# Four mixing-gate units and the two state-gate and four state-projection units move into the attention of a three-block fp32 kernel

## The chip, the cores and the metric

The kernel runs on one core of a Trainium2 chip. The metric is the device time of one execution in microseconds (us). The engines of the core run their own instruction queues side by side and wait for one another on semaphores: TensorE (PE) multiplies matrices, VectorE (DVE), ScalarE (ACT) and GpSimd (POOL) work elementwise, SyncE (SP) issues the weight loads.

## The reference

Input is a sequence of 256 tokens of width 1024, all in fp32. The change lies in the first block:

```
h   = rmsnorm(x);  hp = h @ w_in        # u | q | kv | gate logits | 2 x 1024 mixing gates
y_ssm = s5_mixer(u)                     # 32 groups x 64 complex states, a scan over 256 tokens,
                                        # then gelu, and out = yg * sigmoid(yg @ w_glu + b_glu)
y_nsa = nsa_mixer(q, kv, gate logits)   # 8 heads, 2 kv groups: compressed (15 blocks),
                                        # selected and windowed attention, three softmaxes
gate  = sigmoid(mixing gates)
merged = gate[0] * (y_ssm @ w_proj_ssm) + gate[1] * (y_nsa @ w_proj_nsa)
x = x + merged @ w_out
x = x + relu(rmsnorm(x) @ w_up)**2 @ w_down
```

Two more layers follow (feed-forward, retention or latent attention, memory attention, feed-forward); only the product of the memory with its key and value weights (`mem_w_kv_2`, here `w_mem`) is computed already in the first block. The change touches nothing behind the first block.

## The kernel before

**Units.** All weights come in units of up to 1 MB, in the order of the list `UNITS`; SP loads unit n into slot n mod 4 of `raw` as soon as unit n-4 is used up. A split unit is multiplied in three passes so that the result has fp32 accuracy: ACT rounds the weights into `whi` (line 582), DVE subtracts to get `wlo` (line 1033), and PE multiplies high by high, low by high and high by low (line 1825, 48 matmuls of 256 columns for a full unit, 24 for a half unit such as `w_glu`, `w_ps`, `w_pn`). `whi` and `wlo` have two slots each, so the splitting of a unit waits until the unit two before it is multiplied. `ensure` and `ahead` in ACT's and DVE's queues write these splits into the queues by hand. `w_mem` and `w_c1` units aren't split. PE writes unit results in turn into banks 0 and 1 of PSUM, and DVE empties them (`fill_result`).

**State loop.** 16 state tiles j, in 8 pairs p. Per tile DVE turns the inputs by cosine and sine (lines 1179, 1180), adds (`zin`, lines 1213, 1214), scans (`zz`, line 1218), and POOL turns the two scans back in four products (`pr`, lines 1742, 1743). PE does `inputs(p+1)` (line 1942), then `outputs(p-1)` (line 1953), which waits until POOL is through with both tiles of the pair before; POOL may start the next pair only behind these outputs. Between them PE has one unit per tile (`fill(FILL[j])`): 16 of them, the second `w_q`, three `w_kv`, eight `w_mg` (mixing gates), four `w_mem`. `keys_values` (lines 1970 to 1977) stands before the last fill.

**Between loop and attention.** PE compresses the blocks of keys and values (line 2004), computes the gate logits (line 2016) and small products, then `w_glu` 0 and 1 on `yghi`/`yglo`, waits for the sigmoid and the split of the gated output (`yshi`, `yslo`, line 1270), and multiplies the four `w_ps`.

**Attention.** 12 parts (`sub`) of 4 heads each, in groups of three (selected, windowed, compressed), and `values` behind each group (line 2074). PE's order is: scores of part k+2, transposes of part k, values. DVE reads the scores (`prep`: lines 1292, 1297, 1303), ACT takes the exponentials (line 745), DVE normalises (`norm`), PE transposes, ACT copies to SBUF (`copies`, line 755). Scores have one set of banks, so scores of the next part wait until `prep` has read those before. Parts 0 to 5 belong to the first 128 queries (128 keys), parts 6 to 11 to the second (256 keys). After it `yshi`, `yslo` are made from the attention output, and the four `w_pn` units and `w_out` follow.

Of the kernel before, what the change touches and what calls it, by code (L numbers as in the profile page):

```python
# [6 lines left out]
F32 = mybir.dt.float32  # L7
# [4 lines left out]
P = 128  # L12
# [46 lines left out]
def unit_list():  # L59
# [40 lines left out]
AT = {(u[0], u[1]): n for n, u in enumerate(UNITS)}  # L100
NOT_GROUP = ("w_dn", "w_fd", "w_out", "w_o", "w_c1")
# [143 lines left out]
def program(nc, A, out):  # L245

    ctx = ExitStack()
    with ctx:
# [53 lines left out]
        sS = sb("sS", [P, 2, 4 * T], where=[at_yT[0]])  # L302
# [8 lines left out]
        QK = sb("QK", [P, 6, T], where=w)  # L311
        VT = sb("VT", [P, 2, T], where=w)
        KC = sb("KC", [P, 2, T], where=w)
        at_tokens = [w[0]]
        mg = sb("mg", [P, 16, T], where=w)
        xtok = sb("xtok", [P, TT, D], where=at_tokens)
# [24 lines left out]
        yg = sb("yg", [P, 4, T], where=at_ahi)  # L341
        sg = sb("sg", [P, 4, T], where=at_ahi)
        yghi = sb("yghi", [P, 4, T], F32R, where=at_alo)
        yglo = sb("yglo", [P, 4, T], F32R, where=at_alo)
# [17 lines left out]
        cpart = sb("cpart", [P, P], where=at_small)  # L362
        w[0] += 4 * 6 * T
        assert at_small[0] <= w[0]
        sdk = sb("sdk", [P, 2, T], where=w)
        assert w[0] == mark + 3 * half_turn
        mrg = sb("mrg", [P, KT, T], where=w)
        alibi = sb("alibi", [P, NH, T], where=w)
        alibc = sb("alibc", [P, TT, NH, 16], where=w)
        maskc = sb("maskc", [P, TT, HG, 16], where=w)  # L370
        gate = sb("gate", [P, TT, 24], where=w)
# [63 lines left out]

        FILL = {j: AT["w_q", 1] + j for j in range(N_STATE_TILES)}
        assert FILL[N_STATE_TILES - 1] == AT["w_mem", 3]

# [19 lines left out]
        def pre_gain(q):  # L458
# [3 lines left out]
                     nsa=[(alibi, "alibi"), (alibc, "alibc"), (maskc, "maskc"), (xr, "xt")],  # L462
# [107 lines left out]
        def _(act):  # L570
# [122 lines left out]
            act.wait_ge(S("qk_sums"), 1)  # L693
            nc.scalar.activation(rq[:], PS[6][:, 64:80].rearrange("p (a b c) -> p a b c", a=TT, b=HG), ACT.Sqrt,
                                 bias=V["eps"], scale=1.0 / DH).then_inc(S("qk_root"), 1)
            nc.scalar.activation(sdk[:], two(3), ACT.Sqrt, bias=V["eps"], scale=1.0 / DH).then_inc(S("qk_root"), 1)
# [8 lines left out]

            state_gelu(0)
            ensure(SPLIT_BEFORE[AT["w_glu", 0]], AT["w_c1", 1])
            act.wait_ge(*done(AT["w_c1", 1]))
            nc.scalar.activation(cpart[:], PS[7][:, 0:P], ACT.Copy).then_inc(S("cmp_part"), 1)
            act.wait_ge(S("cmp_sum"), 1)  # L710
# [5 lines left out]
            state_gelu(1)  # L716
            act.wait_ge(S("c_done"), N_STATE_TILES)
            for dst, name in SMALL["nsa"]:
                act.dma_start(dst[:], A[name]).then_inc(S("in_nsa"), 16)
            ensure(SPLIT_BEFORE[AT["w_glu", 0]] + 1, AT["w_c1", 1])  # L720
            act.wait_ge(S("gate_logit"), 1)
            nc.scalar.activation(gate[:], gate[:], ACT.Sigmoid).then_inc(S("gate"), 1)
            for c in range(2):
                ahead(AT["w_glu", c])
                act.wait_ge(S("evac"), GROUP[AT["w_glu", c]] + 1)
                nc.scalar.activation(sg[:, 2 * c:2 * c + 2], sg[:, 2 * c:2 * c + 2], ACT.Sigmoid).then_inc(S("ssm_gate"), 1)
            act.wait_ge(S("ys"), 1)
            nc.scalar.activation(yshi[:], yg[:], ACT.Copy).then_inc(S("yshi"), 1)
# [3 lines left out]
            for c in range(4):  # L732
                ahead(AT["w_ps", c])
# [25 lines left out]
            def attention(steps):  # L759
# [10 lines left out]
            nc.scalar.activation(yshi[:], ynf[:], ACT.Copy).then_inc(S("yshi"), 1)  # L770
            for c in range(4):
                ahead(AT["w_pn", c])
# [249 lines left out]
        def _(dve):  # L1022
# [187 lines left out]
            for j in range(N_STATE_TILES):  # L1210
# [9 lines left out]
                if j:  # L1220
# [3 lines left out]
                if j and UNITS[FILL[j - 1]][3]:  # L1224
# [8 lines left out]
            cp(VV[:], PS[2][:, :].rearrange("p (a b c) -> p a b c", a=2, b=TT)).then_inc(S("vv"), 1)  # L1233
            dve.wait_ge(S("qk_root"), 2)
# [8 lines left out]
            state_low(0)  # L1243
            fill_result(FILL[N_STATE_TILES - 1])
            for k in range(2, 4):
                state_output(k)
            ensure(SPLIT_BEFORE[AT["w_glu", 0]], AT["w_c1", 1])
            state_low(1)
# [10 lines left out]

            ensure(SPLIT_BEFORE[AT["w_glu", 0]] + 1, AT["w_c1", 1])  # L1260
            for c in range(2):
                bank = group(AT["w_glu", c])
# [1165 lines left out]
```

## Time and profile before

| | |
|---|---|
| time, median of 3 runs | 1510.44 us (1507.84 to 1510.45) |
| the profiled execution, its own time | 1510.51 us |
| its span (first to last instruction) | 1508.7 us |
| PE / PE weight load busy | 1418.8 / 1374.0 us |
| DVE / ACT / POOL busy | 927.9 / 724.3 / 194.4 us |
| granted TensorE clock, mean | 0.967 of full |

The profile names for each wait what ended it; a chain followed back from the last instruction shows which engine set the end at each moment. Matmuls overlap, so a stretch in which PE counts as busy throughout can still be one of matmuls at half clock; the granted clock is given beside it.

### The profile page before, as it was taken

The numbers are of one execution on the slowest core, as the hardware profiler recorded it, in microseconds if no ns is written. First come the engines' busy times: TensorE is split into PE (matmuls) and PEld (weight loads), VectorE is DVE, ScalarE is ACT, GpSimd is POOL, SyncE is SP. The second block draws the span as 40 slices with busy tenths as digits, with TensorE's granted clock in tenths as the row PEclk, the third lists the DMA queues.
The fourth block names the chain that finished last, engine by engine and source line by source line (L and its number), as shares of the span: only waits on it lengthen the run. The fifth ranks groups of instructions, "written<-read, shape, count | busy, mean of one in ns | idle before, by whom it ended". The sixth has DMA issues, their size and how long they took to land.

```text
span 1508.7 us, 28232 instructions
## 1 busy us (share of the span) xinstructions
PE 1418.8 (94%) x11538; PEld 1374.0 (91%) x11538; DVE 927.9 (62%) x1372; ACT 724.3 (48%) x1193; POOL 194.4 (13%) x210
## 2 busy tenths in 40 slices
PE   5899888799999999999998999999999979899998
PEld 5888777799999999998898999999999977899998
DVE  7998666466644665546765656546665475566544
ACT  7722344354433544435544644436444364654443
POOL 0455100002200011104110211002110010111100
PEclk9899977899999999999999999999999989999999
DMA  9332520344555455554343455554555450255551
GB/s 369 112 141 97 195 84 1 112 160 177 193 196 196 151 184 195 192 195 149 140 154 119 161 183 196 193 196 152 183 205 193 175 193 29 84 181 181 209 193 60
DMA packets 36815, 244.33 MB, mean 162 GB/s; under 512 B 4208, under 2 KB 5360, under 8 KB 8816
## 3 DMA queue, kind: packets, MB, share of 16 engines
q1 hardware_dynamic: 34992, 238.17, 43.8%
q10 hardware_dynamic: 1728, 4.81, 0.9%
q8 instruction: 70, 1.15, 0.3%
q14 instruction: 25, 0.20, 0.0%
HBM read 241.67 MB, written 1.05 MB: 161 GB/s over the span
## 4 chain that ended last, share of the span: by engine, by line
PE 84%; DVE 9%; ACT 4%; issue 1%; DMA 1%; SPq 0%; DVEq 0%; ACTq 0%
PE ps L1825 50%; PE ps L1865 25%; DVE wlo L1033 3%; PE ps L2074 2%; PE ps L2048 1%; ACT whi L582 1%; DVE alo L1414 1%; PE ps L1953 1%; DMA xtok<-in_xt 1%; PE ps L2064 1%; DVE sS L1292 1%; ACT junk L784 1%; DVE yr L1392 0%; ACT pP L745 0%; PE ps L1942 0%
## 5 line engine op out<-in xcount | busy, mean ns | idle before, releaser
L1033 DVE TENSOR_TENSOR wlo<-raw,whi 128x1024 fp32r<-128x1024 f32 (+1 forms) x434 | 506.1, 1208 | 288.7 <-ACT whi L582 288.5
L1825 PE MATMUL ps<-ahi,whi 128*128 128x256 f32 x2112 | 601.5, 285 | 31.7 <-DVE wlo L1033 17.6
L582 ACT ACTIVATE whi<-raw 128x1024 fp32r<-128x1024 f32 (+1 forms) x434 | 427.3, 1032 | 413.7 <-PE ps L1825 217.4
L1825 PE MATMUL ps<-alo,whi 128*128 128x256 f32 x2112 | 596.2, 282 | 0.0
L1825 PE MATMUL ps<-ahi,wlo 128*128 128x256 f32 x2112 | 595.4, 282 | 0.0
L1825 PEld LDWEIGHTS ps<-ahi,whi 128*128 128x128 f32 x2112 | 403.7, 191 | 39.6 <-issue 25.2
L1825 PEld LDWEIGHTS ps<-alo,whi 128*128 128x128 f32 x2112 | 402.8, 191 | 0.7 <-issue 0.7
L1825 PEld LDWEIGHTS ps<-ahi,wlo 128*128 128x128 f32 x2112 | 402.8, 191 | 0.0
L1763 POOL TENSOR_TENSOR hlo<-fh,hhi 128x256 f32 (+3 forms) x104 | 85.7, 824 | 762.0 <-ACT hhi L851 540.9
L1474 DVE TENSOR_TENSOR fa<-ps,r 128x512 f32<-128x512 f32 x104 | 71.9, 692 | 174.3 <-PE ps L1825 174.1
L1865 PE MATMUL ps<-whi,hhi 128*128 128x256 f32 x960 | 147.9, 276 | 0.0
L1865 PE MATMUL ps<-wlo,hhi 128*128 128x256 f32 x960 | 147.9, 276 | 0.0
L1865 PE MATMUL ps<-whi,hlo 128*128 128x256 f32 x960 | 147.8, 276 | 0.0
L1865 PEld LDWEIGHTS ps<-whi,hhi 128*128 128x128 f32 x960 | 126.7, 188 | 0.0
L1865 PEld LDWEIGHTS ps<-whi,hlo 128*128 128x128 f32 x960 | 126.7, 188 | 0.0
L1865 PEld LDWEIGHTS ps<-wlo,hhi 128*128 128x128 f32 x960 | 126.7, 188 | 0.0
L851 ACT ACTIVATE hhi<-fh 128x256 f32 (+1 forms) x88 | 36.8, 418 | 135.1 <-DVE fh L1481 135.1
L1775 POOL TENSOR_TENSOR xr<-xr,yr 128x512 f32<-128x512 f32 x20 | 24.8, 1273 | 327.7 <-PE ps L1885 327.7
L1742 POOL TENSOR_TENSOR pr<-zz,cosT 128x256 f32<-128x256 f32 x32 | 30.7, 958 | 98.9 <-PE ps L1953 58.0
L1481 DVE TENSOR_TENSOR fh<-fs,fa 128x256 f32<-128x256 f32 x88 | 36.9, 419 | 1.9 <-ACT fs L848 1.9
L848 ACT ACTIVATE fs<-fa 128x256 f32<-128x256 f32 x88 | 35.3, 401 | 4.9 <-DVE fa L1474 4.9
L797 ACT ACTIVATE ahi<-ps,vecs 128x128 fp32r<-128x128 f32 x112 | 29.5, 412 | 7.8 <-PE ps L1895 7.8
(344 smaller groups left out, 1392.8 us busy)
## 6 DMA issues: line engine op xcount, KB each, us to landing
raw<-in_w_gu SPq DMA_DIRECT2D x88, 1024.0 KB, 4.8
raw<-in_w_fd SPq DMA_DIRECT2D x44, 1024.0 KB, 4.8
raw<-in_w_up SPq DMA_DIRECT2D x16, 1024.0 KB, 4.8
raw<-in_w_dn SPq DMA_DIRECT2D x16, 1024.0 KB, 4.8
raw<-in_w_ret SPq DMA_DIRECT2D x13, 1024.0 KB, 4.9
raw<-in_w_mg SPq DMA_DIRECT2D x8, 1024.0 KB, 4.8
raw<-in_w_o SPq DMA_DIRECT2D x8, 1024.0 KB, 6.8
raw<-in_w_mem SPq DMA_DIRECT2D x4, 1024.0 KB, 4.8
```

What stands on the lines that cost most here:

```text
L582: nc.scalar.activation(whi[:, m % SPL, c], raw[:, n % RAW, c], ACT.Copy).then_inc(S("w_hi"), 1)
L797: ins = nc.scalar.activation(ahi[:, k, t * P:t * P + P], PS[turned(t, h)][:, i * P:i * P + P], ACT.Copy, scale=pre_gain(q)[:, k:k + 1])
L848: nc.scalar.activation(fs[:, b], fa[:, b, 0:T], ACT.Silu).then_inc(S("silu"), 1)
L851: nc.scalar.activation(dst, fh[:, b, 0:T], ACT.Copy).then_inc(S("hid_hi"), 1)
L1033: ins = tt(wlo[:, m % SPL, c], raw[:, n % RAW, c], whi[:, m % SPL, c].bitcast(F32), ALU.subtract)
L1474: tt(fab, two((g0 + u) % 2), over(r[:, 0:T], 2), ALU.mult).then_inc(S("evac"), 1)
L1481: tt(fh[:, b, 0:T], fs[:, b], fa[:, b, T:2 * T], ALU.mult).then_inc(S("hidden"), 1)
L1742: tt(pr1[:, b, s], zz[:, b, s], cosT[:, j], ALU.mult).then_inc(S("turned"), 1)
L1763: tt(dst, src, high.bitcast(F32), ALU.subtract).then_inc(S("hid_lo"), 1)
L1825: ins = mm(dst, lhsT, rhs, start=k == 0 and p == 0, stop=k == kt - 1 and p == len(pairs) - 1)
L1865: ins = mm(two(2 + 2 * t + c // 2)[:, c % 2], x[:, k, xs], wgt[:, n_slot(n), ws], start=u + kk + p + c % 2 == 0, stop=u == n_units - 1 and ...
L2074: ins = mm(PS[v["bank"]][rows, slot * P:slot * P + P], lhsT, rhs, start=k == 0, stop=k == len(terms) - 1)
```

## The change

It reorders `UNITS` (4 of the 8 `w_mg` and the last `w_mem` go behind), gives 11 instead of 16 tiles of the state loop a unit (`FILL_TILES`: tiles 0 to 4, 6, 8, 10, 11, 12, 14), and puts the others into the attention: `w_mem` 3 between the scores of parts 0 and 1; a table `BESIDE` names the unit that PE multiplies behind the transposes of a part: `w_glu` at parts 0 and 1, `w_ps` at 4 to 7, `w_mg` 4 to 6 at 8 to 10; `w_mg` 7 stands behind the last values. DVE and ACT handle a unit of part n-1 at part n (`beside(n)`). The sigmoid of the state gate reads PSUM directly on ACT. Buffers move to free others (`sS` to the place that `xr` takes later), so that the load of `xr` (`small_in("res")`) now follows the attention, and a wait for it stands ahead of `yslo` on DVE. Functions before the attention on ACT are reordered, with activations on a dummy element that load the next function table (`warm_root`, and those on `warm`).

```
-    add("w_mg", 0, 8)
-    add("w_mem", 0, 4, split=False)
+    add("w_mg", 0, 4)
+    add("w_mem", 0, 3, split=False)
     add("w_c1", 0, 2, split=False)
+    add("w_mem", 3, 1, split=False)
     add("w_glu", 0, 2, 1024)
     add("w_ps", 0, 4, 1024)
+    add("w_mg", 4, 4)
...
+BESIDE = {0: ("w_glu", 0), 1: ("w_glu", 1), 4: ("w_ps", 0), 5: ("w_ps", 1), 6: ("w_ps", 2), 7: ("w_ps", 3),
+          8: ("w_mg", 4), 9: ("w_mg", 5), 10: ("w_mg", 6)}
+FILL_TILES = (0, 1, 2, 3, 4, 6, 8, 10, 11, 12, 14)
...
# ACT
+            act.wait_ge(S("turned"), 4 * N_STATE_TILES)
+            small_in("bias")
...
+            def ssm_gates():
+
+                for c in range(2):
+                    n = AT["w_glu", c]
+                    act.wait_ge(*done(n))
+                    bank = two(GROUP[n] % 2)
+                    for t in range(2):
+                        k = 2 * c + t
+                        ins = nc.scalar.activation(sg[:, k], bank[:, t], ACT.Sigmoid, bias=V["b_glu"][:, k:k + 1])
+                    ins.then_inc(S("evac"), 1)
+
+            def beside(n):
+
+                if n == 0:
+                    ensure(SPLIT_BEFORE[AT["w_glu", 0]] + 1, AT["w_c1", 1])
+                if n - 1 in BESIDE:
+                    ahead(AT[BESIDE[n - 1]])
+                if n == 2:
+                    ssm_gates()
+                if n == 3:
+                    act.wait_ge(S("ys"), 1)
+                    nc.scalar.activation(yshi[:], yg[:], ACT.Copy).then_inc(S("yshi"), 1)
...
                     if n + 1 < len(todo):
                         exps(todo[n + 1])
+                    beside(n)
                     copies(s)
...
             nc.scalar.activation(yshi[:], ynf[:], ACT.Copy).then_inc(S("yshi"), 1)
+            small_in("res")
+            ahead(AT["w_mg", 7])
+            for c in range(4, 8):
+                mix_sigmoid(c)
...
# DVE
+            def beside(n):
+
+                if n == 0:
+                    fill_result(AT["w_mem", 3])
+                    ensure(SPLIT_BEFORE[AT["w_glu", 0]] + 1, AT["w_c1", 1])
+                if n - 1 in BESIDE:
+                    name, c = BESIDE[n - 1]
+                    if name == "w_mg":
+                        fill_result(AT[name, c])
+                    if name == "w_ps":
+                        tt(mrg[:, 2 * c:2 * c + 2], ready(AT[name, c]), mg[:, 2 * c:2 * c + 2], ALU.mult).then_inc(S("evac"), 1)
+                    ahead(AT[name, c])
...
             attention(parts["nsa"], 0)
+            dve.wait_ge(S("in_res"), 16)
             dve.wait_ge(S("yshi"), 2)
             tt(yslo[:], ynf[:], yshi[:].bitcast(F32), ALU.subtract).then_inc(S("yslo"), 1)
+            fill_result(AT["w_mg", 7])
...
# PE
-            pe.wait_ge(S("yglo"), 2)
-            unit(AT["w_glu", 0], yghi, yglo, GLU_KT)
+            outputs(N_STATE_TILES // 2 - 1)
             pe.wait_ge(S("kc_sq"), 1)
...
-            unit(AT["w_glu", 1], yghi, yglo, GLU_KT)
-            pe.wait_ge(S("yslo"), 1)
-            for c in range(4):
-                unit(AT["w_ps", c], yshi, yslo, GLU_KT)
...
                         if k < len(todo):
                             scores(todo[k])
                         transposes(s)
+                        beside(k - 2)
                     else:
                         values(s)
```

The first place is PE's queue in the state loop, the pair of tiles 6 and 7; a unit is shown by its first matmul, `L1942` are the inputs of the next pair, `L1953` the outputs of the pair before. Before:

```order
L1942 MATMUL ps<-uT,BT 128x256 [waits bu_read]
...
L1825 MATMUL ps<-ahi,whi 128x256 [waits w_lo,evac]
...
L1953 MATMUL ps<-pr_96,CD 32x256 [waits turned]
...
L1825 MATMUL ps<-ahi,whi 128x256 [waits w_lo,evac]
...
L1942 MATMUL ps<-uT,BT 128x256 [waits bu_read]
```

After, in the same pair (lines 1993, 1876 and 2004 are the same calls):

```order
L1993 MATMUL ps<-uT,BT 128x256 [waits bu_read]
...
L1876 MATMUL ps<-ahi,whi 128x256 [waits w_lo,evac]
...
L2004 MATMUL ps<-pr_99,CD 32x256 [waits turned]
...
L1993 MATMUL ps<-uT,BT 128x256 [waits bu_read]
```

The unit behind the outputs is gone, so that inputs of the next pair follow the outputs at once.

The second place is DVE's queue at tiles 9 and 10, from the read-out of a mixing-gate unit (`mg`) on. Before:

```order
L1173 TENSOR_TENSOR mg<-ps,r 128x512
L1179 TENSOR_TENSOR t_98<-ps,cosT 128x512
L1180 TENSOR_TENSOR t_99<-ps,sinT 128x512
L1033 TENSOR_TENSOR wlo<-raw,whi 128x1024 x2
L1213 TENSOR_TENSOR zin<-t_98,t_99 128x256
L1214 TENSOR_TENSOR zin<-t_98,t_99 128x256
L1218 SCALAR_TENSOR_TENSOR zz<-sv,zin 128x256 x2
L1173 TENSOR_TENSOR mg<-ps,r 128x512
```

After:

```order
L1215 TENSOR_TENSOR mg<-ps,r 128x512
L1221 TENSOR_TENSOR t_101<-ps,cosT 128x512
L1222 TENSOR_TENSOR t_102<-ps,sinT 128x512
L1255 TENSOR_TENSOR zin<-t_101,t_102 128x256
L1256 TENSOR_TENSOR zin<-t_101,t_102 128x256
L1260 SCALAR_TENSOR_TENSOR zz<-sv,zin 128x256 x2
L1221 TENSOR_TENSOR t_101<-ps,cosT 128x512
```

The weight split and the next read-out are gone from this stretch; of the splits of this loop behind tile 5 one is left, at tile 7.

The third place is PE's queue in the attention, parts 8 to 10 (`L2048` or `L2099` scores, `L2064` or `L2115` transposes, `L2074` or `L2125` values). Before:

```order
L2048 MATMUL ps<-QK 128x256 [waits att_read]
...
L2064 MATMUL ps<-tabs,PC 128x128 [waits att_copy,att_prob]
L2074 MATMUL ps<-pTs,VV 64x128 [waits att_out,att_copy]
...
L2048 MATMUL ps<-kcr,QK 128x15 [waits att_read]
...
L2064 MATMUL ps<-tabs,pP 128x128 [waits att_copy,att_prob]
```

After:

```order
L2099 MATMUL ps<-QK 128x256 [waits att_read]
...
L2115 MATMUL ps<-tabs,PC 128x128 [waits att_copy,att_prob]
L1876 MATMUL ps<-ahi,whi 128x256 [waits w_lo,evac]
...
L2125 MATMUL ps<-pTs,VV 64x128 [waits att_out,att_copy]
...
L2099 MATMUL ps<-kcr,QK 128x15 [waits att_read]
...
L2115 MATMUL ps<-tabs,pP 128x128 [waits att_copy,att_prob]
...
L1876 MATMUL ps<-ahi,whi 128x256 [waits w_lo,evac]
```

A full mixing-gate unit now stands between the transposes of a part and the values, and another behind the transposes of the next part.

## Rows read from the trace of the kernel before

**Rows 1.** The page: engines of the chain that ended last.

```profile
PE 84%; DVE 9%; ACT 4%; issue 1%; DMA 1%; SPq 0%; DVEq 0%; ACTq 0%
```

**Rows 2.** Busy time by stretch (start:end, length, engines, clock, DMA share, GB/s).

```profile
70.98:156.88 85.90, 85.90 (x609) 74.23 (x610) 77.86 (x108) 22.41 (x28) 39.76 (x40) 0.96 0.37 128
156.88:205.00 48.12, 40.58 (x338) 37.45 (x337) 25.89 (x45) 18.45 (x31) 6.43 (x11) 0.86 0.44 153
205.00:270.52 65.52, 51.90 (x278) 44.12 (x277) 42.42 (x120) 30.69 (x116) 0.00 (x0) 0.77 0.09 33
270.52:290.91 20.39, 13.37 (x96) 13.11 (x97) 14.03 (x22) 9.92 (x12) 0.00 (x0) 0.86 0.50 176
```

**Rows 3.** The chain in order of time, state loop (start us, us, what).

```profile
94.06 1.85 PE ps L1953 x16
95.91 5.86 PE ps L1825 x48
101.76 1.06 PE ps L1942 x8
...
132.07 7.10 PE ps L1825 x32
```

**Rows 4.** The timeline of DVE, tiles 8 and 9 (start us, us, instruction).

```profile
100.10 0.96 DVE L1213 TENSOR_TENSOR zin<-t,t 128x256 f32<-128x256 f32 x1
...
105.86 2.34 DVE L1033 TENSOR_TENSOR wlo<-raw,whi 128x1024 fp32r<-128x1024 f32 x2
108.13 0.41 DVE L1213 TENSOR_TENSOR zin<-t,t 128x256 f32<-128x256 f32 x1
...
110.10 0.67 DVE L1173 TENSOR_TENSOR mg<-ps,r 128x512 f32<-128x512 f32 x1
...
114.73 0.96 DVE L1213 TENSOR_TENSOR zin<-t,t 128x256 f32<-128x256 f32 x1
```

**Rows 5.** The timeline of POOL, first and last of eight products of tiles 6 and 7.

```profile
95.98 0.74 POOL L1742 TENSOR_TENSOR pr<-zz,cosT 128x256 f32<-128x256 f32 x1 [5.68 <-PE ps L1953]
...
103.58 1.12 POOL L1743 TENSOR_TENSOR pr<-zz,sinT 128x256 f32<-128x256 f32 x1
```

**Rows 6.** The timeline of PE around tile 2's unit.

```profile
52.50 0.36 PE L1825 MATMUL ps<-ahi,whi 128*128 128x256 f32 x1 [2.18 <-DVE wlo L1033]
...
53.50 0.41 PE L1825 MATMUL ps<-alo,whi 128*128 128x256 f32 x1
53.71 0.41 PE L1825 MATMUL ps<-ahi,wlo 128*128 128x256 f32 x1
```

**Rows 7.** Busy time of two stretches of small products behind the loop.

```profile
156.88:160.12 3.24, 3.24 (x24) 2.76 (x24) 0.69 (x1) 0.00 (x0) 3.16 (x5) 1.00 0.24 99
167.03:175.39 8.36, 8.36 (x137) 7.19 (x137) 4.04 (x9) 2.75 (x7) 0.00 (x0) 1.00 0.81 261
```

**Rows 8.** The timeline of ACT, a table load between two activations.

```profile
188.17 1.06 ACT L728 ACTIVATE yshi<-yg 128x1024 fp32r<-128x1024 f32 x1 [1.29 <-DVE yg L1268]
189.24 1.28 ACT L730 ACT_TABLE_LOAD   x1
190.53 0.27 ACT L730 ACTIVATE kcr<-ps,vecs 128x15 f32<-128x15 f32 x1
```

**Rows 9.** The chain in order of time, `w_ps` and the attention's end.

```profile
190.53 14.54 PE ps L1825 x96
...
267.42 0.71 DVE ynf L1326
268.15 1.06 ACT yshi L770
269.24 1.24 DVE yslo L1348
```

**Rows 10.** DMA issues (issuer, count, KB each, us to landing).

```profile
alibi<-in_alibi ACTq DMA_DIRECT2D x1, 1024.0 KB, 4.9
xr<-in_xt ACTq DMA_DIRECT2D x1, 1024.0 KB, 7.9
```

More of the change, by code:

```diff
@@ L362, in program @@
         cpart = sb("cpart", [P, P], where=at_small)
+        alibc = sb("alibc", [P, TT, NH, 16], where=at_small)
+        maskc = sb("maskc", [P, TT, HG, 16], where=at_small)
+        gate = sb("gate", [P, TT, 24], where=at_small)
         w[0] += 4 * 6 * T
@@ L366, in program @@
         assert w[0] == mark + 3 * half_turn
+        alibi = sb("alibi", [P, NH, T], where=w)
+        assert w[0] == mark + 4 * half_turn
         mrg = sb("mrg", [P, KT, T], where=w)
[L368 to L371, printed above, removed]
         end_nsa = w[0]
@@ L715, in _ @@
             ins.then_inc(S("hid"), 1)
[L716 to L720, printed above, removed]
+            act.wait_ge(S("turned"), 4 * N_STATE_TILES)
+            small_in("bias")
             act.wait_ge(S("gate_logit"), 1)
             nc.scalar.activation(gate[:], gate[:], ACT.Sigmoid).then_inc(S("gate"), 1)
[L723 to L728, printed above, removed]
+            warm_root()
             act.wait_ge(S("kc_sums"), 1)
@@ L731, in _ @@
               .then_inc(S("kc_root"), 1)
-            for c in range(4):
-                ahead(AT["w_ps", c])
+            chain(nc.scalar.activation(warm[:], V["eps"], ACT.Gelu_apprx_tanh))
+            state_gelu(1)
+            chain(nc.scalar.activation(warm[:], V["eps"], ACT.Exp))
+            def ssm_gates():
[17 more added lines that the diff above has]
+                    nc.scalar.activation(yshi[:], yg[:], ACT.Copy).then_inc(S("yshi"), 1)
             def exps(s):
@@ L1258, in _ @@
             chain(ins)
-            ensure(SPLIT_BEFORE[AT["w_glu", 0]] + 1, AT["w_c1", 1])
-            for c in range(2):
-                bank = group(AT["w_glu", c])
-                for t in range(2):
-                    k = 2 * c + t
-                    ins = ts(sg[:, k], bank[:, t], V["b_glu"][:, k:k + 1], None, ALU.add)
-                ins.then_inc(S("evac"), 1)
-            dve.wait_ge(S("ssm_gate"), 2)
-            tt(yg[:], yg[:], sg[:], ALU.mult).then_inc(S("ys"), 1)
-            dve.wait_ge(S("yshi"), 1)
-            tt(yslo[:], yg[:], yshi[:].bitcast(F32), ALU.subtract).then_inc(S("yslo"), 1)
+            for k in range(2, 4):
+                state_output(k)
             dve.wait_ge(S("kc_root"), 1)
@@ L1274, in _ @@
                 .then_inc(S("kc_ready"), 1)
-            for c in range(4):
-                bank = group(AT["w_ps", c])
-                dve.wait_ge(S("mix_gate"), 8)
-                tt(mrg[:, 2 * c:2 * c + 2], bank, mg[:, 2 * c:2 * c + 2], ALU.mult).then_inc(S("evac"), 1)
             dve.wait_ge(S("gate"), 1)
-            dve.wait_ge(S("in_nsa"), 64)
+            dve.wait_ge(S("in_bias"), 16)
+            dve.wait_ge(S("in_block_bias"), 32)
+            dve.wait_ge(S("mix_gate"), 4)
+            def beside(n):
[9 more added lines that the diff above has]
+                    ahead(AT[name, c])
+                if n == 3:
+                    dve.wait_ge(S("yshi"), 1)
+                    tt(yslo[:], yg[:], yshi[:].bitcast(F32), ALU.subtract).then_inc(S("yslo"), 1)
             def prep(s):
@@ L1341, in attention @@
                             late = None
+                        beside(k - 1)
                     else:
@@ L1984, in _, with gate_logits @@
                     inputs(p + 1)
-                fill(FILL[2 * p])
+                if 2 * p in FILL:
+                    fill(FILL[2 * p])
                 if p:
                     outputs(p - 1)
-                if p == N_STATE_TILES // 2 - 1:
-                    keys_values()
-                fill(FILL[2 * p + 1])
+                if 2 * p + 1 in FILL:
+                    fill(FILL[2 * p + 1])
+            keys_values()
+            def gate_logits(t):
+                for k in range(KT):
+                    ins = mm(PS[4][:, 32 + 24 * t:56 + 24 * t], xg[:, k, t * P:t * P + P], wg24[:, k, :],
+                             start=k == 0, stop=k == KT - 1)
+                if t:
+                    ins.then_inc(S("gates_done"), 1)
             pe.wait_ge(S("cx"), 1)
@@ L2012, in _ @@
             ins.then_inc(S("cmp_sum"), 1)
[L2013 to L2018 removed]
+            gate_logits(1)
             pe.wait_ge(S("hid"), 1)
@@ L2089, in attention, with beside @@
                         transposes(s)
+                        beside(k - 2)
                     else:
                         values(s)
+            def beside(n):
+                if n in BESIDE:
+                    name, c = BESIDE[n]
+                    if name == "w_mg":
+                        fill(AT[name, c])
+                    elif name == "w_glu":
+                        pe.wait_ge(S("yglo"), 2)
+                        unit(AT[name, c], yghi, yglo, GLU_KT)
+                    else:
+                        pe.wait_ge(S("yslo"), 1)
+                        unit(AT[name, c], yshi, yslo, GLU_KT)
             pe.wait_ge(S("qk_ready"), 1)
-            pe.wait_ge(S("kc_ready"), 1)
             attention(parts["nsa"])
+            fill(AT["w_mg", 7])
             pe.wait_ge(S("yslo"), 2)
```

75 lines of the change are left out of this document (44 added, 31 removed).

## The prediction, made before the kernel ran

> **What bounds the kernel now.** I read the chain first: PE sets the end for 84% of the span [rows 1], so a change counts by what it does to PE's queue, or to what PE waits for. Next come four stretches cut at the places that the change touches [rows 2]. In the state loop from 70.98 to 156.88 us PE counts as busy all the time at a clock of 0.96, and the chain in order of time [rows 3] shows nothing but PE there: a unit of 48 matmuls takes 5.86 us, a memory unit (32 matmuls) 7.10, outputs 1.85, inputs 1.06. A pair of tiles costs 2 x 5.86 + 1.85 + 1.06 = 14.63 us. DVE is only just behind: from `zin` of tile 8 to `zin` of tile 10 are 114.73 - 100.10 = 14.63 us too [rows 4], and it hardly pauses. The stretch 156.88 to 205.00 holds small products, `w_glu` and `w_ps`, with PE busy 40.6 of 48.1 us. The attention, 205.00 to 270.52, is bound by the chain through scores, DVE, ACT and back: PE busy 51.9 of 65.5 at a clock of 0.77, DVE 42.4, ACT 30.7. So in the loop PE has too much, in the attention it has gaps and a low clock.
>
> The sum is made against the profiled execution (span 1508.7, its own time 1510.51, which is the median of 1510.44 within 0.1 us).
>
> **Term 1, the state loop: -16.4 us.** Up to the outputs of the first pair, which end at 81.5, units and order are the same. Behind them units leave at tiles 5, 7, 9, 13 and 15, and the units of tiles 6 to 12 are renamed (mixing gates 1 to 3, then memory 0 and 1). PE now has 5.86 + 1.85 + 1.06 = 8.8 us a pair. Three things can be late next. DVE: 14.63 less a split (2.34) and a read-out (0.6) [rows 4] is 11.7, and 9.3 where the second split is gone too; this is so from tile 8 on. POOL: its eight products took 103.58 + 1.12 - 95.98 = 8.7 us [rows 5], and since POOL waits for the outputs and the outputs for POOL, a pair can't be shorter than 8.7 + 1.85 = 10.6. That is my price of a pair with one unit: between 8.8 (PE alone) and 11.7 (DVE with a split). Hand count by queue order: outputs(2) can start at 81.6 + 8.7 = 90.3 and end at 92.1; inputs until 93.2; unit 8. PE has waited 2 us there, and such a gap of 2.18 us was followed by matmuls 0.21 us apart (53.50 to 53.71 [rows 6]) instead of the 5.86 / 48 = 0.12, the lower of the two clock levels; so I give unit 8 8.5 us instead of 5.9. It ends at 101.7, outputs(3) at 103.6, unit 10 at 110.5, outputs(4), waiting for POOL, at 113.1. Then memory 0, inputs, memory 1: 7.1 + 1.06 + 7.1 = 128.4; outputs(5) 130.2; memory 2 until 137.3; outputs(6) wait for POOL (130.2 + 8.6 = 138.8) and end at 140.5. Before they ended at 156.88. Bounds: if DVE's 11.7 counts in three pairs, 3 us less; if no matmul runs at the low clock, 1.5 us more.
>
> **Term 2, end of the loop to the first scores: -33.2 us.** Before: 205.0 - 156.9 = 48.1. `w_glu`, the wait for the gate, and `w_ps` leave (they are paid in term 3), as does the memory unit. What remains on PE is 3.24 of `keys_values` and the 8.36 of small products [rows 7] with the last outputs among these: 11.6. Into this go waits for ACT, which has to do gelu, the two roots, gelu again and so on, with a table load of 1.28 us [rows 8] at each switch; in my count PE waits some 1 us for `cmp_part` and 1.5 for `hid`, and the rest is gaps of tenths. The first scores start at 140.5 + 14.9 = 155.4. Neither the read of `alibi` (4.9 us [rows 10], issued some 3 us ahead of its need at `prep`) nor the root of the compressed keys holds PE, since memory 3 stands behind the first scores and covers 7.1 us.
>
> **Term 3, first scores to the first `w_pn`: +41.7 us.** Before 65.5. PE's own attention work is 51.9 us busy at a clock of 0.77 [rows 2], so about 40 at full clock. Added: memory 3 7.1; six half units at 5.86 / 2 = 2.93, so 17.6; four mixing-gate units 23.4. Together 88. By the queue order DVE and ACT keep up: with a full unit beside it a part takes PE 2.0 scores + 1.1 transposes + 5.9 = 9.0 us, DVE 3.1 `prep` + 1.6 `norm` + 0.7 + 2.34 for result and split, 7.7; DVE's total is 42.4 + some 25 of splits, read-outs and state-gate work = 67, ACT's 31 + some 20 = 51. A unit of part n-1 is done before ACT and DVE reach `beside(n)`, so the splits queue nobody up. What stays as waits of PE: 1.5 until the first exponentials; about 4 at part 2, where ACT does the split, a load for sigmoid (1.28), four sigmoids of PSUM and only then the copies that the first `values` wait for; about 3 at part 4, whose scores wait for the read behind yg x sg, `yshi`, `yslo`; 1.5 in between. And about 3 at the end: `xr` is now loaded behind the attention, DVE's `yslo` waits for it, and everything behind `yslo` on DVE with it. From the last values 0.71 + 1.06 [rows 9] + 0.65 issue + 4.9 (a lone 1 MB, rows 10; 7.9 in company) + 1.24 = 8.6, of which the last mixing-gate unit covers 5.86. So 88 + 13 = 101. The clock is dearer to guess: the second half, parts 5 to 11, is nearly unbroken PE work as in the loop (0.96), the first half has the gaps. I add 6 us: 107.2. Bounds: 0 extra gives 101; a clock of 0.77 over all 88 us gives 88 / 0.77 = 114, so with the waits 127.
>
> **Term 4, `w_pn` to `w_out`: 0.** 20.4 us in both [rows 2]. ACT's four sigmoids and a table load (3.8 us) now stand ahead of the split of `w_pn` 2, which waits for `w_pn` 0 anyway; `w_pn` 0 took until 275.1 of a start at 270.5, 4.6 us, so they hide; if that cover is gone it is at most 2. Nothing later changes.
>
> Sum: -16.4 - 33.2 + 41.7 = -7.9, so 1502.6 us.
>
> **A rule weighed against the rows.** Rows 8 show ACT finishing at 189.23, a load from 189.24 for 1.28 us, and the next activation at 190.53: 1.28 us a switch, nothing else. The Trainium skill, "ScalarE: Activation LUTs", section "What ACT_TABLE_LOAD costs", has each switch at 1.28 us and a drain of about 1.38 on top. With five switches of the changed kernel on the path the sum by it would be 5 x 1.38 = 6.9 us more, 1509.5.
>
> **The rivals.**
> (A) The forecast, 1498 to 1507.4: 0.50.
> (B) More gain: PE at full clock nearly throughout, hence without the 6 us and the 1.5 in the loop: 1495. For it: in the loop outputs and inputs between units left the clock at 0.96. Against: gaps of 2 us and more. 1490 to 1498: 0.18.
> (C) The gain is eaten by waits: the pair in the loop is held by DVE (+3) and `xr` comes in company of weight loads (7.9 instead of 4.9, +3): 1508.6. Nothing in rows 10 excludes it. 0.09. The change doing nothing in the loop, because POOL and DVE hold the pair at 14.6 anyway, is excluded by the 8.7 us of POOL [rows 5].
> (D) Slower: the clock. If PE stays at the attention's old 0.77 through all added units, the stage from first scores to `w_pn` takes 127 instead of 107.2 us and the kernel 1522. It is slower than before from a stage of 115 us on, which is a mean clock of 88 / 102 = 0.86. For it: 0.77 was measured with PE busy 79% of the time, so being busy alone did not lift it; against: those were products of 64 rows or columns, and the added are full ones. 1514 to 1524: 0.17. On this bears the Trainium skill, "TensorE: Matmul & The Clock Gate", section "HAM oscillation — how this bites in real kernels": work that comes in bursts between waits starts each burst at the low clock, every time. By that, with full units at the low level, the time would be that of this rival, 1522; the trace agrees [rows 6].
> (E) Each table switch costs more than the load in rows 8, where ACT had nothing queued behind it; if it is another load's length, the five on the path cost 5 x 1.28 = 6.4 us more and the time is 1509. Against it: the gap of 0.01 us in rows 8. 0.06. (The page on ScalarE named above would give 1509.5.)
>
> **How the numbers follow.** The likeliest is A, its middle 1502.6. To hold 8 of 10, the range reaches from inside B (1494) over C and E to 1514, the lower end of D. A measurement of this kernel can tell about 0.2%, 3 us, from no change. Faster than 1507.4: A and B, 0.68. Same: C and E, 0.15. Slower: D, 0.17.
>
> **What the profile of the changed kernel would show.** Term 1: the last outputs in the loop end near 140.5, pairs about 10.6 long with PE waiting for POOL's `pr` ahead of the outputs. Were PE to wait for DVE's `zz` or `wlo` instead, DVE is the bound. Term 2: first scores near 155. Term 3: `w_pn` starts near 262.6, clock in the stage about 0.9; a wait of PE for `yslo` of some 3 us ahead of `w_pn` 0 with the DMA of `xr` behind it; a wait for ACT's `pTs` ahead of the first values. Term 4: 20 us to `w_out`. Wrong it would be by a clock under 0.86 in the attention, by PE waiting for DVE beside full units, or by a wait for a weight load there.

## The result and the profile after

| | before | after |
|---|---|---|
| median of 9 runs each, side by side | 1508.24 us (1506.44 to 1512.17) | 1495.34 us (1489.16 to 1502.57) |
| ratio, 95% interval | | 0.9915 (0.9901 to 0.9928) |
| profiled span | 1508.7 us | 1492.3 us |
| PE clock, mean | 0.967 | 0.974 |

The kernel became 12.9 us faster; 7.9 were forecast. Of all executions below one, of 5163 us in a variant (`xr` late, sigmoids early), was in a slow state; its median counts it, the ratios don't. The page of the kernel after, busy time of the engines and the engines of the chain (beside [rows 1]):

```profile
PE 1408.5 (94%) x11538; PEld 1362.4 (91%) x11538; DVE 925.4 (62%) x1368; ACT 731.1 (49%) x1204; POOL 193.0 (13%) x210
...
PE 80%; DVE 10%; ACT 4%; issue 2%; DMA 1%; POOL 1%; SPq 0%; DVEq 0%; ACTq 0%; POOLq 0%
```

PE's busy time fell by 10 us with the same work, 7.0 of them ahead of `w_out`: fewer of its matmuls ran at the low clock, as the clocks below show. The same stretches as in [rows 2], with the attention cut once more at part 6 (start:end, length, then busy time of PE, PE weight load, DVE, ACT, POOL, the clock, DMA share, GB/s):

```profile
70.98:141.35 70.37, 64.50 (x416) 51.91 (x416) 62.56 (x91) 11.96 (x17) 38.81 (x42) 0.93 0.29 99
141.35:159.55 18.20, 18.20 (x161) 13.86 (x161) 12.59 (x23) 10.71 (x17) 5.80 (x10) 0.63 0.41 136
159.55:194.49 34.94, 27.45 (x167) 24.84 (x166) 23.26 (x66) 22.52 (x64) 0.00 (x0) 0.90 0.30 106
194.49:257.99 63.50, 60.87 (x480) 57.17 (x480) 43.99 (x91) 30.47 (x86) 0.00 (x0) 1.00 0.29 100
257.99:277.07 19.08, 12.03 (x97) 11.65 (x97) 15.81 (x25) 13.27 (x17) 0.00 (x0) 0.88 0.68 245
```

| term | forecast | measured | off by |
|---|---|---|---|
| 1, state loop (before to 156.88, after to 141.35) | -16.4 | -15.5 | +0.9 |
| 2, to the first scores (48.1, now 18.2) | -33.2 | -29.9 | +3.3 |
| 3, to the first `w_pn` (65.5, now 98.4) | +41.7 | +32.9 | -8.8 |
| 4, to `w_out` (20.4, now 19.1) | 0 | -1.3 | -1.3 |
| sum | -7.9 | -13.8 | -5.9 |

Behind the start of `w_out`, where nothing was changed, the profiled spans have 1217.8 us before and 1215.2 after; another execution of the kernel after has 1221.6 (below). Such differences are the spread between executions and no effect. The point at which the loop ends has such a spread too (below), so the first row of the table is known only to some us.

The loop. PE's timeline, outputs of two pairs (start us, us, instruction, in brackets the idle time before it and what ended it):

```profile
91.11 3.24 PE L2004 MATMUL ps<-pr,CD 128*32 128x256 f32 x16 [1.93 <-POOL pr L1794]
...
103.16 1.06 PE L2004 MATMUL ps<-pr,CD 128*32 128x256 f32 x8 [1.58 <-POOL pr L1794]
```

PE waits for POOL's `pr`, as forecast. The outputs start at 80.35, 91.11, 103.16 and 111.96 us: pairs of 10.8, 12.1 and 8.8 us, where 14.63 stood before. At the loop's end DVE is late instead, in its own timeline:

```profile
129.19 0.88 DVE L1209 TENSOR_SCALAR mv<-ps,rm 128x256 f32<-128x256 f32 x2 [4.18 <-PE ps L1876]
```

It waits 4.18 us for the second memory unit, which PE multiplies from 122.05 on, and its work for the compressed blocks stands behind that read-out. PE in turn waits 1.40 us for it before `keys_values`. What follows is the chain of the kernel after (start us, us, what):

```profile
140.70 0.61 DVE t L1222
...
141.35 0.66 PE ps L2021 x4
142.01 2.42 PE ps L2027 x16
144.43 1.92 PE ps L2028 x2
146.34 3.48 PE ps L2064 x64
```

PE counts as busy for all of the 18.20 us, but at a clock of 0.63.

The attention. What PE waited for from 141 to 258 us (waits: us in total, times, longest):

```profile
PE ps L2125 <- ACT pTs L792: 5.3, 2, 3.9
PE ps L2099 <- DVE sS L1333: 2.7, 2, 1.4
PE ps L2021 <- DVE t L1222: 1.4, 1, 1.4
PE ps L1876 <- DVE yslo L1396: 1.3, 1, 1.3
```

The waits stand where they were forecast: 3.9 us ahead of the first values, 1.4 ahead of the scores of part 6 behind `yslo`, 1.3 at the end for `xr`. From part 6 on PE is busy 60.87 of 63.50 us at full clock.

### The profile page after: what moved, and what is told of

Same layout as the page of the kernel before. It is cut to its first block, busy times and chain, and to the rows that moved or that the text cites. A ratio compares the mean times of both kernels' runs of the same rounds, so it can differ in the third digit from the quotient of the medians.

```text
span 1492.3 us, 28244 instructions
## 1 busy us (share of the span) xinstructions
PE 1408.5 (94%) x11538; PEld 1362.4 (91%) x11538; DVE 925.4 (62%) x1368; ACT 731.1 (49%) x1204; POOL 193.0 (13%) x210
## 4 chain that ended last, share of the span: by engine, by line
PE 80%; DVE 10%; ACT 4%; issue 2%; DMA 1%; POOL 1%; SPq 0%; DVEq 0%; ACTq 0%; POOLq 0%
PE ps L1876 48%; PE ps L1916 26%; DVE wlo L1075 3%; PE ps L2125 1%; PE ps L2099 1%; ACT whi L592 1%; DVE alo L1465 1%; DMA xtok<-in_xt 1%; PE ps L2115 1%; POOL pr L1793 1%; ACT junk L826 1%; POOL pr L1794 1%; PE ps L2004 0%; ACT pP L782 0%; DVE yr L1443 0%
```

## Experiments

Time and ratio stand against runs of the kernel before on the same chip. "Stage" is first scores to first `w_pn`.

**The kernel after once more**, no edit.

> The changed kernel once more, as the measure for the runs beside it and for the spread of its stages. Every theory expects a ratio to the kernel before of 0.990 to 0.993 and the first scores between 155 and 160 us.

Measured: 1493.52 us, ratio 0.9898 (0.9875 to 0.9921). Its profiled execution has 18.3, 98.5 and 19.0 us in the stretches of terms 2 to 4, as the first one (18.2, 98.4, 19.1), and 6.4 us more behind them. So these stages repeat to some 0.1 us in the two, and the whole is to be trusted to 2 or 3.

The loop repeats less well. Six of the variants below (gates behind, gates early, exponential, both with `xr` late, product late) multiply the same units in the same order up to the first scores. Their `keys_values` start between 136.99 and 140.41 us, against 141.35 and 140.56 here, and their first scores between 154.17 and 158.63, against 159.55 and 158.93. A shift of a few us ahead of the attention therefore shows nothing by itself. Differences to the kernel after are taken below from its first ratio, 0.9915; against this one each variant would look 2.6 us worse.

**All eight mixing gates in the loop.**

```
-    add("w_mg", 0, 4)
+    add("w_mg", 0, 8)
...
-    add("w_mg", 4, 4)
...
-          8: ("w_mg", 4), 9: ("w_mg", 5), 10: ("w_mg", 6)}
-FILL_TILES = (0, 1, 2, 3, 4, 6, 8, 10, 11, 12, 14)
+FILL_TILES = tuple(range(15))
```

> The changed kernel with all eight mixing-gate units back in the state loop (15 tiles have a unit) and only w_mem 3, w_glu and w_ps beside the attention. Theory (units in the loop cost their full 5.86 us, beside the attention part of a unit falls into gaps, and the last one covers the wait for yslo): the last outputs in the loop end near 156.9 as before, the stage from first scores to w_pn takes about 85 us instead of 98.4, and the whole is 2 to 4 us slower than the changed kernel, about 1498. Rival 1 (the whole gain is the mixing gates' move): 1508, as before. Rival 2 (moving them gained nothing, all of it came from w_glu and w_ps filling gaps): 1492 or less.

Their sigmoids and read-outs move with them, and `yghi`, `yglo` to another buffer. Measured: 1496.65 us, ratio 0.9931 (0.9908 to 0.9954). Loop end to first scores, then the stage:

```profile
155.50:170.20 14.70, 13.59 (x163) 10.66 (x161) 8.56 (x16) 10.67 (x17) 6.92 (x11) 0.88 0.50 181
170.20:257.25 87.05, 70.42 (x454) 63.31 (x453) 57.40 (x146) 45.48 (x141) 0.00 (x0) 0.89 0.24 79
```

Against the kernel after, the four units (23.4 us of work) make the loop 14.1 us longer (up to 18.5, with the spread above) and the stage 11.4 shorter, and 3.5 more is saved between the two (14.7 against 18.2). `w_pn` starts at 257.25 and 257.99, `w_out` at 278.13 and 277.07. So the move of the four gates that names the change is worth 1.1 us up to `w_out` and 2.4 us by the ratios (1.8 and 5.0 against the kernel after once more), less than their intervals settle. Most of the gain lies in what this variant keeps: `w_glu`, `w_ps` and the memory unit beside the attention, and ACT's functions in their new order. No run here takes these apart.

**The gates behind the attention.**

```
+BESIDE = {0: ("w_glu", 0), 1: ("w_glu", 1), 4: ("w_ps", 0), 5: ("w_ps", 1), 6: ("w_ps", 2), 7: ("w_ps", 3)}
...
-            fill(AT["w_mg", 7])
+            for c in range(4, 8):
+                fill(AT["w_mg", c])
```

> w_mg 4 to 6 no longer stand beside parts 8 to 10 but, with w_mg 7, behind the attention. Theory (parts 8 to 11 without a unit are bound by the chain over DVE and ACT, about 23 us instead of 32.5): attention 7 to 10 us shorter, 16.9 us more PE work behind it, less the 1.4 us of waiting: 5 to 8 us slower than the changed kernel, about 1502. Rival (a unit beside a part costs its full time, since the parts are bound by PE anyway): no difference.

Splits and read-outs move with the units. Measured: 1500.73 us, ratio 0.9960 (0.9946 to 0.9974), 6.8 us above the kernel after. The two halves of its stage:

```profile
156.60:237.45 80.85, 67.70 (x454) 61.10 (x453) 57.69 (x144) 45.81 (x140) 0.00 (x0) 0.94 0.25 85
237.45:260.10 22.65, 22.65 (x193) 22.65 (x193) 9.91 (x11) 6.23 (x7) 0.00 (x0) 1.00 0.39 132
```

The attention up to its last values takes 80.85 us, against 91.3 (159.55 to 250.88) with three of these units in it. So a unit of 5.86 us of work costs 3.5 there (10.5 / 3) and its full time behind it.

**Dummy matmuls in the attention of the kernel before.** It adds work (24 matmuls of unused results behind each of 11 transposes).

```
                         transposes(s)
+                        if s["index"] < 11:
+                            pe.wait_ge(S("evac"), GROUP[AT["w_ps", 3]] + 1)
+                            for i in range(24):
+                                mm(two(0)[:, i % 2], yshi[:, i % 4, 0:P], yslo[:, i // 6], start=True, stop=True)
```

> The kernel before, with 24 useless matmuls (0.12 us each at full clock, 2.9 us a part) behind the transposes of parts 0 to 10 of its attention, and nothing else; the output is untouched. Theory (PE's gaps take up part of the added work, and full matmuls lift the clock of the attention from 0.77 to above 0.9): 31.7 us of work are added and the stage 205 to 270.5 grows by 10 to 16 us only. Rival (the clock stays at 0.77 and the parts are bound by PE): 31.7 / 0.77 = 41 us longer.

Measured: 1523.82 us, ratio 1.0112 (1.0086 to 1.0138). Its stage:

```profile
202.72:282.26 79.54, 72.06 (x541) 66.95 (x541) 42.52 (x120) 30.87 (x116) 0.00 (x0) 0.96 0.08 28
```

264 matmuls at 5.86 / 48 are 32 us of work, the stage is 14.0 longer. Against [rows 2] the clock rose from 0.77 to 0.96, and PE's busy time by only 20: by this difference the attention's own matmuls take 72 - 32 = 40 us then, not 52. This refutes rival D and supports the 40 of the sum.

**Gates 4 and 5 beside parts 2 and 3**, to fill the wait at part 2.

```
     add("w_glu", 0, 2, 1024)
+    add("w_mg", 4, 2)
     add("w_ps", 0, 4, 1024)
-    add("w_mg", 4, 4)
+    add("w_mg", 6, 2)
...
+BESIDE = {0: ("w_glu", 0), 1: ("w_glu", 1), 2: ("w_mg", 4), 3: ("w_mg", 5), 4: ("w_ps", 0), 5: ("w_ps", 1), 6: ("w_ps", 2), 7: ("w_ps", 3),
+          8: ("w_mg", 6)}
```

> w_mg 4 and 5 stand beside parts 2 and 3, where nothing stood, instead of two of the three full units at parts 8 to 10. Theory (parts 8 to 11 are bound by PE, parts 2 to 4 by the chain over DVE and ACT with PE idle): 11.3 us leave the dense half, some 5 come back in the first: 4 to 6 us faster than the changed kernel, near 1490. Rival (the first half is bound by DVE and ACT, which get two read-outs and full splits, 2.9 and 2.0 us each): no gain, or up to 3 us slower.

Measured: 1498.88 us, ratio 0.9946 (0.9931 to 0.9960): 4.7 us slower than the kernel after. PE's timeline at part 2, and the stretch of parts 9 to 11:

```profile
184.35 0.58 PE L1877 MATMUL ps<-ahi,whi 128*128 128x256 f32 x1 [4.61 <-ACT sg L758]
```

```profile
234.00:260.90 26.90, 21.27 (x155) 19.69 (x153) 10.78 (x27) 9.87 (x27) 0.00 (x0) 0.87 0.29 98
```

The unit needs the bank that the sigmoid of the state gate has yet to read, so the wait is only moved ahead of it (4.61 instead of 3.9), and the last parts stand bare. The stage takes 105.3 us, 6.8 more than in the kernel after; the 4 to 6 us of gain that were expected did not come.

**The wait for `xr` moved behind the splits of `w_out`.**

```
             attention(parts["nsa"], 0)
-            dve.wait_ge(S("in_res"), 16)
...
                 ahead(AT["w_out", c])
+            dve.wait_ge(S("in_res"), 16)
```

> DVE's wait for the load of xr moves from ahead of yslo to ahead of the first use of xr, behind the splits of w_out. Theory (term 3: about 3 us of PE wait hang on it; in the trace 1.4 us were seen between the end of w_mg 7 and w_pn 0): 1.4 us less, PE goes from w_mg 7 to w_pn 0 without a pause. Rival: DVE's read-out of w_mg 7 and the split are late anyway, no difference.

Measured: 1490.37 us, ratio 0.9891 (0.9873 to 0.9909). The chain:

```profile
249.20 5.86 PE ps L1876 x48
...
256.32 1.28 ACT L697
...
259.81 0.53 ACT whi L592
...
262.38 3.15 PE ps L1876 x24
```

`w_pn` 0 starts at 254.89 without a pause, but `w_pn` 2 then waits for its split, which ACT makes behind the four sigmoids: last values to `w_out` take 26.2 us as before the edit. First `w_pn` to `w_out` takes 20.5 us instead of 19.1: here is what term 4 put at "if that cover is gone at most 2". The interval overlaps both intervals of the kernel after.

**The same, with three of the sigmoids ahead of the split of `w_pn` 1.**

```
-            ahead(AT["w_mg", 7])
-            for c in range(4, 8):
+            for c in range(4, 7):
                 mix_sigmoid(c)
+            ahead(AT["w_mg", 7])
+            mix_sigmoid(7)
```

> As the run with the late wait for xr, and ACT does the sigmoids of w_mg 4 to 6 ahead of the split of w_pn 1 instead of behind it. Theory (the late wait took PE's pause ahead of w_pn 0 away, but w_pn 2 then waited for its split behind ACT's table load and four sigmoids, 20.5 us instead of 19.0 to w_out): with ACT's work in the shadow of w_mg 7 the stretch from the last values to w_out shrinks by 1.5 to 3 us against the changed kernel (26.2 us). Rival: the split of w_pn 1 is late instead, no difference.

Measured: 1490.23 us, ratio 0.9888 (0.9870 to 0.9906). The chain now has one unbroken piece from `w_mg` 7 through `w_pn` 2:

```profile
247.35 14.66 PE ps L1877 x120
```

Last values to `w_out`: 24.5 us, 1.6 less. In the whole this is too small to show.

**Exponential instead of sigmoid for the state gate**, so that the gate's values are those of another function. No table switch is needed.

```
-                        ins = nc.scalar.activation(sg[:, k], bank[:, t], ACT.Sigmoid, bias=V["b_glu"][:, k:k + 1])
+                        ins = nc.scalar.activation(sg[:, k], bank[:, t], ACT.Exp, bias=V["b_glu"][:, k:k + 1])
```

> The sigmoid of the state gate in the attention is replaced by the exponential, so that the two table loads around it (to sigmoid and back) fall away; the state gate's values are another function. Theory (a switch costs its 1.28 us load; one of the two loads lies on the chain at part 2, the second in the shadow of DVE): 1.3 us less from first scores to w_pn. Rival (a switch costs twice its load, rival E): 2.6 us or more. Rival 2 (other waits end there anyway): 0.

Measured: 1494.57 us, ratio 0.9923 (0.9897 to 0.9948). The chain of the kernel after at this place, then that of the experiment:

```profile
182.84 1.04 ACT whi L592 x2
...
183.90 1.28 ACT L757
185.18 0.01 issue
185.19 0.03 ACT sg L757
...
194.49 1.99 PE ps L2099 x8
```

```profile
177.76 0.61 ACT whi L592
178.38 1.45 ACT sg L757 x4
...
187.55 3.78 PE ps L2099 x8
...
192.37 3.73 PE ps L1876 x24
```

Without the load the scores of part 6 come 33.4 instead of 34.9 us behind the first scores, 1.5 earlier (34.8 to 34.9 in five traces of the code with the load): hardly more than the load's 1.28. The Trainium skill, "ScalarE: Activation LUTs", section "What ACT_TABLE_LOAD costs", has a drain of about 1.38 us on top; this trace shows 0.02 and 0.01 us around the load, so here the measurement decides against it. But the whole gained nothing: those scores now run at the low clock, 3.78 us instead of 1.99, and the stage is 100.0 us. That the earlier start caused this isn't shown: PE waited ahead of them as long as in the kernel after (1.44 and 1.43 us), and in the run with only `xr` late, which has the same code up to there, `w_ps` 0 behind them took 4.16 us instead of 2.87.

**The product of the state gate put behind the normalisation of part 3**, to shorten the same wait.

```
-                        if k == 4:
-                            dve.wait_ge(S("evac"), GROUP[AT["w_glu", 1]] + 1)
-                            tt(yg[:], yg[:], sg[:], ALU.mult).then_inc(S("ys"), 1)
...
                         norm(s)
+                        if k == 4:
+                            dve.wait_ge(S("evac"), GROUP[AT["w_glu", 1]] + 1)
+                            tt(yg[:], yg[:], sg[:], ALU.mult).then_inc(S("ys"), 1)
```

> DVE multiplies yg by the gate behind prep of part 4 and norm of part 3 instead of ahead of them. Theory (the chain from part 2 to part 6 runs over ACT's split, table load and sigmoids, DVE's product, prep 4, the exponentials, yshi, yslo and prep 5): DVE's wait of 2.1 us for the sigmoids is filled, scores of part 6 come 2 us earlier, 1 to 2 us less in all. Rival (PE at the low clock gives it back, as in the run with the exponential): no difference in the whole.

Measured: 1492.54 us, ratio 0.9899 (0.9882 to 0.9916). The scores of part 6 come 34.4 instead of 34.9 us behind the first, the stage has 98.0 instead of 98.4: nothing that a run can tell.

**POOL relieved in the loop**: its sine products cover 16 columns, and PE reads the cosine products in their place, so the state output's sine terms are left out of the result.

```
-                    tt(pr2[:, b, s], zz[:, b, s], sinT[:, j], ALU.mult).then_inc(S("turned"), 1)
+                    tt(pr2[:, b, part * T:part * T + 16], zz[:, b, part * T:part * T + 16], sinT[:, j, 0:16], ALU.mult).then_inc(S("turned"), 1)
```

> POOL's sine products in the state loop are cut from 256 to 16 columns and PE reads the cosine products in their place, so the state output is wrong by that; PE and DVE do the same work as in the changed kernel. POOL needs some 5 us a pair instead of 8.7. Theory (term 1: POOL's products and the outputs in turn hold a pair at 10.6): pairs go down to PE's 8.8 to DVE's 9.3, the first scores start 3 to 5 us earlier. Rival (DVE holds the pairs, in its own work or its reads beside POOL): less than 2 us, or only as far as DVE's instructions get shorter without POOL beside them.

Measured: 1488.13 us, ratio 0.9860 (0.9832 to 0.9887). Outputs start at 75.36, 84.11, 92.88 and 101.78 us: pairs of 8.8 to 8.9, PE's own 8.8 of the forecast. PE no longer waits for POOL, so POOL did set the two pairs of 10.8 and 12.1. The first scores come at 146.10, 12.8 to 13.4 us earlier than in the two profiled executions of the kernel after, and 8.1 to 12.5 earlier than in the six variants of the same code; 3 to 5 were expected. Of the 13.4 only 5.2 lie in the three pairs. 5.0 lie ahead of 75.36, where the forecast had POOL hold nothing, and 3.3 behind the pairs. Whether DVE's instructions gain from a lighter POOL was not taken apart. The stage gives back 6:

```profile
146.10:250.50 104.40, 94.71 (x646) 87.51 (x645) 67.45 (x156) 53.49 (x150) 0.00 (x0) 0.90 0.28 96
```

With as many matmuls (646, and 167 + 480 in the kernel after) PE counts as busy for 94.7 us instead of 88.3.

**The second memory unit at tile 13 instead of 12.**

```
-FILL_TILES = (0, 1, 2, 3, 4, 6, 8, 10, 11, 12, 14)
+FILL_TILES = (0, 1, 2, 3, 4, 6, 8, 10, 11, 13, 14)
```

> The unit w_mem 1 moves from tile 12 to tile 13 of the state loop, behind the outputs of the pair before, so that DVE reads it out behind the block inputs and doesn't wait 4.2 us for it ahead of them. Theory (the tail of the loop is bound by DVE, which waits for w_mem 1 and then has 12 us of work): keys_values start 1 to 3 us earlier. Rival (PE then is the bound with w_mem 1 and 2 in a row): no difference.

Measured: 1486.32 us (1485.29 to 1487.73), ratio 0.9865 (0.9846 to 0.9884), whose interval lies clear of the first one of the kernel after, but not of the second (0.9875 to 0.9921); by the ratios it gains 7.5 or 5.0 us. The chain, and the stretch from loop end to first scores:

```profile
122.89 14.01 PE ps L1876 x64
136.90 1.85 PE ps L2004 x16
138.75 0.59 PE ps L2021 x4
139.34 1.68 PE ps L2027 x16
141.02 0.97 PE ps L2028 x2
141.99 1.92 PE ps L2064 x64
```

```profile
138.75:152.31 13.56, 13.56 (x161) 10.45 (x161) 8.46 (x16) 10.73 (x17) 6.93 (x11) 0.87 0.52 194
```

PE comes to `keys_values` without the 1.40 us wait. The same 161 matmuls, counted as busy throughout in both, take 13.56 us at 0.87 instead of 18.20 at 0.63 (13.60 in the run with all four edits).

This is not the clock alone. The run with only `xr` late has the code of the kernel after up to the first scores, and a higher clock in this stretch, yet it is no shorter. Its stretch, and what PE waited for in it:

```profile
137.94:156.59 18.65, 16.13 (x161) 12.83 (x161) 12.49 (x23) 10.77 (x17) 5.84 (x10) 0.73 0.42 133
```

```profile
147.57 1.12 PE L2072 MATMUL ps<-tabs,cpart 128*128 128x64 f32 x4 [2.51 <-ACT cpart L728]
```

ACT's write of `cpart` in the run with `xr` late, and in this one (in the kernel after it starts at 150.65):

```profile
147.24 0.28 ACT L728 ACTIVATE cpart<-ps 128x128 f32<-128x128 f32 x1
```

```profile
143.99 0.28 ACT L728 ACTIVATE cpart<-ps 128x128 f32<-128x128 f32 x1 [0.40 <-PE ps L2064]
```

Against the start of `keys_values` (137.94, 138.68 and 141.35 us in PE's timeline) `cpart` starts 9.3, 5.3 and 9.3 us later, and 9.3 too in the kernel after once more and the other variants of that code. ACT gets there behind DVE's last tile, `uT`, and two table loads, so PE could multiply `cpart` (`L2072`) only from 9.6 us on, at either clock. At tile 13 DVE is ahead, and ACT waits for PE instead. Up to that product PE needs 7.0 us instead of 10.2, from it to the first scores 6.6 instead of 7.9.

**Four of these edits together** (`xr` late, sigmoids early, product late, tile 13).

> The three edits above together with the late wait for xr. Theory: their gains add up to 3 to 6 us below the changed kernel, near 1489. Rival: every microsecond won ahead of a stretch at the low clock is given back, within 1.5 us of the changed kernel.

Measured: 1486.46 us, ratio 0.9869 (0.9842 to 0.9896), the same as tile 13 alone. Last values to `w_out` are 24.6 us again, but the stage has 98.75. Tile 13 alone is the version to keep: one number changed, 21 us faster than the kernel before by the medians, against 13 to 14 without it.

## Why the prediction was right, and where its sizes were off

The total lies inside the range (1494 to 1514) but below the likeliest rival A (1498 to 1507.4), since a term too cheap by 3.3 us and one too dear by 8.8 cancel in part.

**Term 1 held** to 0.9 us. The mechanism was reasoned, the closeness is partly luck: traces of the same code end the loop anywhere from 137.0 to 141.4 us. The queue count said outputs(4) end at 113.1, outputs(5) at 130.2 and the last outputs at 140.5; they ended at 113.9, 131.0 and 140.0. (By its own 8.7 us of POOL the count should have read 103.6 + 8.7 + 1.85 = 114.1, and 1.0 us more for all that stands behind.) That POOL and the outputs take turns is shown twice, by PE's waits of 1.93 and 1.58 us and by the lighter POOL. But 10.6 is no floor: the next eight products took 6.8 us instead of 8.7, that pair was 8.8 long, and neither these outputs nor the last ones waited. The 2.6 us that unit 8 was given for the low clock fell on the outputs ahead of it (3.24 instead of 1.85 us) and on the next wait for POOL; unit 8 took 5.9. What the count did not have is the 1.40 us wait for DVE ahead of `keys_values`.

**Term 2 was too cheap by 3.3 us.** Two steps are too small: "3.24 of `keys_values` and the 8.36 of small products", taken from a stretch at a clock of 1.00 [rows 7], and the wait of "some 1 us for `cmp_part`". The small products ran at 0.63 here. But they had to wait for ACT's `cpart` in any case: at 0.73 the same code took 18.65 us, with PE idle for 2.51 (over all eight traces of that code the stretch takes 16.6 to 18.7). So up to that product the low clock hides the wait and costs 10.2 - 9.6 = 0.6 us; the rest of the miss is ACT's and DVE's time ahead of `cpart`, and the low clock behind it. Tile 13 shortens both parts, by 3.2 and 1.3 us, and comes out 1.3 below the forecast 14.9.

**Term 3 was too dear by 8.8 us**, and this step set the miss: "I add 6 us" for the clock, and 13 us of waits. PE is busy 27.45 + 60.87 = 88.3 us, against 88 counted at full clock, so the 6 us were not spent on top of it. (The low clock did cost something in the first half, where `w_glu` 0 took 4.38 us and `w_ps` 0, as many matmuls, 2.87 behind it; that lies inside the 88.3, so the count of 88 had some slack.) PE idles 10.1 instead of 13 (3.9 of the 4 at part 2, 1.4 of the 3 at part 4, 1.3 of the 3 for `xr`). `xr` took 5.04 us from 251.64, not 7.9 in company (rival C). The filler run shows why 0.77 was the wrong measure: between full products the attention's own ones run faster. The argument that the second half is nearly unbroken PE work as in the loop stood in the text, and its clock was 1.00; the 6 us did not follow from it.

**Term 4** got 1.3 us. The cover of ACT's sigmoids held; the late wait for `xr` shows what lies under it.

Of the rivals, B (full clock, 1490 to 1498) describes the time of 1495.3 and the cause in the attention; between loop and scores the clock was low and the time longer than forecast. C is excluded by the 5.04 us and by PE waiting for POOL and not DVE in the pairs, D by the filler run and by the stage's own 98.4 us, E by the exponential for the one load that it removes; the two loads ahead of `cpart` show the same gaps of 0.01 to 0.02 us.

**The name of the change and its gain.** The gates' own move gives 1 to 5 us, which the intervals don't settle; most of the gain is there without it. That their place matters the other two variants show: behind the attention 6.8 us slower, under its first half 4.7.

## What to carry to other kernels

Price filler work between waiting parts at its full-clock time minus the gaps it fills, and reprice the old small products at the higher clock too; the clock of the bare stage is no measure for the filled one. Where small products follow a loop, look at which engine has to finish its last tile first, and at the unit order just ahead: one tile's difference let DVE and ACT be ready 4.0 us earlier and gave 5.0 to 7.5 us. Price such a stretch by the later of two times, PE's at the clock it will have and that of the engines that feed it; a busy PE at the low clock can hide a wait. Measure the spread of each stage over several traces of the same code before reading 1 us out of two of them. Where a stage is shortened ahead of another wait, read the next stage's busy time as well, since it may give the gain back.

## What the hardware showed unexpectedly

- "Busy" says little without the clock, and the clock little without the waits. The same 161 matmuls counted as busy for 18.20 us at 0.63, for 16.13 of 18.65 us at 0.73 and for 13.56 at 0.87, and single pieces doubled (1.92 against 0.97, 3.48 against 1.92). Ahead of them stood a wait of 1.40 us in the first two, and in the third 14.01 us of memory units with outputs on either side.
- The low clock came and went between executions of the same code: in five traces of the same code up to there, `w_ps` 0 at part 6 took 2.87 us in four and 4.16 in one, and the whole loop moved by 4.4 us.
- Time saved ahead of the attention was in part given back in it: with POOL relieved 6 of the 12.8 us (stage 104.4 instead of 98.4, at 0.90). At tile 13 the stage is 1.5 us longer too (99.91), but that is a `w_ps` 0 of 4.36 us, which the run with `xr` late has without anything saved. What brings the low clock back is open.
- The Trainium skill, "TensorE: Matmul & The Clock Gate", section "HAM oscillation — how this bites in real kernels", says that bursts behind long enough waits start at the low clock, every time. The scores of part 6 agree in one run and not in the other: behind 1.44 and 1.43 us of waiting they took 3.78 us (exponential) and 1.99 (kernel after). That full units between them lift the clock, 0.77 to 0.96, is what the filler run shows.
